# Products of constants in twelve pauses of TensorE, joins moved behind them, and one PSUM bank held aside in block 2

## The reference

```
# block 1: modulation from c, then
h = rms_norm(x) * (1 + sc1) + sh1
proj = h @ w_in                          # attention, GLA and gate parts
att = sliding_window_sink_attention(...) # 8 heads, 2 kv heads, window 128
o = gla_chunked(...)                     # gated linear attention, 4 heads
x = x + gt1 * rms_norm(concat(att, o) @ w_out)
h = rms_norm(x) * (1 + sc2) + sh2
x = x + gt2 * rms_norm(moe_ffn(h))       # 32 experts, top 4
# block 2
z = rmsnorm(x) @ w_in                    # 24 chunks of 128 columns
y_a = rglru_group(...)                   # convolution and linear recurrence
y_b = hgrn2_group(...)                   # gated recurrence, 6 heads of 64, decay per channel
y_c = shortconv_group(...)
x = x + concat(y_a, y_b, y_c) @ w_out
x = x + conv_ffn(rmsnorm(x)); x = x + sigmoid(x @ ple_w_gate) * (p @ ple_w_proj)
x = rmsnorm(x)
# block 3, two layers: swiglu, chunked gMLP or sparse attention (nsa), swiglu, each with a layer norm
```

## Time and profile before

| | |
|---|---|
| median of three runs | 2882.8 us (2879.93 to 2883.49) |
| the profiled execution | 2879.23 us, its span 2877.4 us |
| mean granted clock | 0.963 |
| PE busy | 2691.2 us, 94% of the span |
| DVE busy | 1366.8 us, 48% |
| ACT busy | 941.1 us, 33% |
| DMA | 713.64 MB, mean 248 GB/s |

### The profile page before, as it was taken

How to read it: one execution, slowest core, us unless ns; L and a number is a source line. 1 busy time by engine, 2 the same in 40 slices (tenths; PEclk the granted TensorE clock), 3 DMA queues, 4 the chain that set the end, 5 groups by cost and what they waited for, 6 DMA issues and landing times. The chain is left out here.

```text
span 2877.4 us, 39681 instructions
## 1 busy us (share of the span) xinstructions
PE 2691.2 (94%) x16538; PEld 1868.0 (65%) x16538; DVE 1366.8 (48%) x1958; ACT 941.1 (33%) x1243; POOL 223.4 (8%) x160
## 2 busy tenths in 40 slices
PE   7888999999999999967799989999999999999998
PEld 5654333333233332257699889899889899898897
DVE  3563212222212222267677665566575665664655
ACT  4333111111111111144454443444343444425433
POOL 1200000000000000000000010054020010102200
PEclk9977999999999999988899999999999999989999
DMA  8546999999999999943245556455456466440453
GB/s 289 188 162 254 417 418 416 389 406 416 418 417 382 404 418 416 416 143 112 98 162 191 176 183 200 152 191 176 166 194 200 147 205 199 141 161 31 161 193 115
DMA packets 292703, 713.64 MB, mean 248 GB/s; under 512 B 15587, under 2 KB 189369, under 8 KB 259430
## 3 DMA queue, kind: packets, MB, share of 16 engines
q1 hardware_dynamic: 281168, 690.27, 64.4%
q10 hardware_dynamic: 9734, 17.02, 1.8%
q0 software_dynamic: 1616, 3.74, 0.4%
HBM read 709.93 MB, written 1.05 MB: 247 GB/s over the span
## 5 line engine op out<-in xcount | busy, mean ns | idle before, releaser
L370 DVE TENSOR_TENSOR lo<-ring,hi 128x2048 fp32r<-128x2048 f32 x251 | 597.3, 2384 | 303.7 <-ACT hi L361 303.6
L1818 PE MATMUL bank<-expert,xg 128*64 128x512 f32 x2176 | 510.8, 603 | 23.4 <-DMA expert<-in_w_mlp 22.4
L361 ACT ACTIVATE hi<-ring 128x2048 fp32r<-128x2048 f32 x251 | 475.5, 1897 | 151.1 <-PE bank L639 125.3
L431 PE MATMUL bank<-x_hi,hi 128*128 128x256 f32 x1568 | 382.8, 285 | 0.0
L431 PE MATMUL bank<-x_lo,hi 128*128 128x256 f32 x1568 | 380.2, 281 | 0.0
L1818 PEld LDWEIGHTS bank<-expert,xg 128*64 128x64 f32 x2176 | 142.9, 137 | 315.0 <-issue 269.6
L431 PEld LDWEIGHTS bank<-x_lo,hi 128*128 128x128 f32 x1568 | 295.8, 189 | 2.5 <-issue 1.0
L431 PEld LDWEIGHTS bank<-x_hi,hi 128*128 128x128 f32 x1568 | 294.8, 188 | 3.3 <-issue 1.6
L1915 DVE TENSOR_TENSOR acc<-bank,acc 128x512 f32<-128x512 f32 x136 | 84.4, 682 | 426.6 <-PE bank L1905 426.5
L1888 PE MATMUL bank<-expert,aT 128*64 128x512 f32 x1088 | 244.1, 597 | 3.3 <-DMA expert<-in_w_mlp 3.2
L436 PE MATMUL bank<-x_hi,lo 128*128 128x256 f32 x1568 | 204.0, 282 | 0.0
(11 more groups left out here) (623 smaller groups left out, 3815.7 us busy)
## 6 DMA issues: line engine op xcount, KB each, us to landing
expert<-in_w_mlp SPq DMA_DIRECT2D x384, 1024.0 KB, 16.8
ring<-in_l_ffn_w_in SPq DMA_DIRECT2D x88, 1024.0 KB, 5.1
ring<-in_l_ffn_w_out SPq DMA_DIRECT2D x44, 1024.0 KB, 4.9
ring<-in_w_ada SPq DMA_DIRECT2D x24, 1024.0 KB, 6.5
ring<-in_l_gm_w_in SPq DMA_DIRECT2D x24, 1024.0 KB, 5.1
ring<-in_ffn_w_up SPq DMA_DIRECT2D x22, 1024.0 KB, 5.1
ring<-in_w_in SPq DMA_DIRECT2D x21, 1024.0 KB, 5.4
ring<-in_l_gm_w_out SPq DMA_DIRECT2D x12, 1024.0 KB, 4.9
```

The costliest lines, as they stand in the source:

```text
L361: e.activation(k.half("hi", u), k.slot(j), ACT.Copy).then_inc(*k.up("hi_done"))
L370: e.tensor_tensor(k.half("lo", u), k.slot(k.units[u][0]), k.half("hi", u).bitcast(F32), SUB).then_inc(*k.up("lo_done"))
L431: e.matmul(o, l, r, start=fresh, stop=False, skip_group_check=True)
L1818: i = e.matmul(banks[n][j][h * CAP:(h + 1) * CAP, :], x, W[:, (2 * h + j) * 512:(2 * h + j + 1) * 512], start=c == 0, stop=False, skip_gro ...
```

## The change

`stay_busy_pe` issues n products of the identity with the first 512 (or 448) columns of the constants into a bank that is not in use at that time; they add to no semaphore. They are called fillers below. Their numbers and places:

| place | fillers |
|---|---|
| GLA, level 1, ahead of the wait for the level; ahead of the bank of score (1,1,0) | 2, 7 (of 448 columns, in `mod_bank`) |
| attention, second part of jobs 0 and 1, behind the request of the bank | 6, 4 |
| w_out, ahead of the first unit | 7 |
| norms pre2, mix2, fin2, gm, nsa, behind the request of four banks | 11, 26, 10, 7, 7 |
| HGRN2, behind the wait for "hg in" | 11 |
| HGRN2, level 1, ahead of the wait for the level; ahead of the banks of (1,0,1), (4,0,1), (5,0,1), (6,0,1) | 3, 14, 2, 5, 5 |

The joins post1, post2, fin2, gm and nsa stand behind the fillers now, no longer in front of the requests of banks. In block 2 a bank named `spare` is held from before the first units to the end of the decay scores; one more product closes its use.

```diff
+def stay_busy_pe(k, e, out, n):
+    for _ in range(n):
+        e.matmul(out[:, :], k.cc("ident"), k.t["const"][:, 0:out.shape[1]], start=True, stop=True, skip_group_check=True)
-def turn_rows_pe(k, e, nm, src="unit", done=None):
+def turn_rows_pe(k, e, nm, src="unit", done=None, join=None, busy=0):
     banks = [k.bank(e, nm, "turn", i) for i in range(4)]
+    stay_busy_pe(k, e, banks[0], busy)
+    if join:
+        meet(k, e, PE_, join)
...
             Q, K_ = k.t[f"{nm}qe{li % 2}"], k.t[f"{nm}ke{li % 2}"]
+            stay_busy_pe(k, e, spare, busy.get(li, 0))
             e.wait_ge(*k.dve(nm, "level", li))
         for c in range(n):
             for par in range(2):
                 key = (nm, "score", li, c, par)
+                stay_busy_pe(k, e, spare, busy.get((li, c, par), 0))
                 bank, lo = k.bank(e, *key), par * 64
...
-    decay_pe(k, e, "gla", t["gq"], t["gk"], 2, between)
+    decay_pe(k, e, "gla", t["gq"], t["gk"], 2, between, k.mod_bank[:, 64:512], {1: 2, (1, 1, 0): 7})
...
     bank = k.bank(e, "swa", "pv", job)
+    stay_busy_pe(k, e, bank, (6, 4, 0, 0)[job])
...
+        if i == 0:
+            stay_busy_pe(k, e, acc[0, 0], 7)
         e.wait_ge(*k.dve("mo_parts", "lo", i))
...
-    turn_rows_pe(k, e, "mix2")
+    turn_rows_pe(k, e, "mix2", join="post2", busy=26)
+    k.spare = k.bank(e, "spare", hold=True)
...
     e.wait_ge(*k.dve("hg", "in"))
-    decay_pe(k, e, "hg", t["hq"], t["hk"], 3, between_pe)
+    stay_busy_pe(k, e, k.spare, 11)
+    decay_pe(k, e, "hg", t["hq"], t["hk"], 3, between_pe, k.spare, {1: 3, (1, 0, 1): 14, (4, 0, 1): 2, (5, 0, 1): 5, (6, 0, 1): 5})
+    e.matmul(k.spare[:, :], k.cc("ident"), k.t["const"][:, 0:512]).then_inc(*k.MM("spare"))
+    k.drains[("spare",)] = ("mm_done", k.counts["mm_done"].n)
+    k.release("spare")
...
-    meet(k, e, PE_, "post2")
     block2_pe(k, e)
```

More of the change, by code:

```diff
@@ L814, in decay_act, with decay_pe @@
             between(k, e, li)
-def decay_pe(k, e, nm, q, kk, n, between=None):
+def decay_pe(k, e, nm, q, kk, n, between=None, spare=None, busy={}):
     for li, h in enumerate(LEVELS):
@@ L1456, in mixer_out_pe @@
     acc_free(k, "w_out")
-    meet(k, e, PE_, "post1")
-    turn_rows_pe(k, e, "pre2")
+    turn_rows_pe(k, e, "pre2", join="post1", busy=11)
 def sums_done(k, nm, last=3):
@@ L2532, in conv_ffn_pe @@
     acc_free(k, "ple_gate")
-    meet(k, e, PE_, "fin2")
-    turn_rows_pe(k, e, "fin2")
+    turn_rows_pe(k, e, "fin2", join="fin2", busy=10)
 def conv_ffn_act(k, e):
@@ L2941, in gmlp_pe @@
     acc_free(k, "gm")
-    meet(k, e, PE_, "gm")
-    turn_rows_pe(k, e, "gm")
+    turn_rows_pe(k, e, "gm", join="gm", busy=7)
 def gm_load_act(k, e):
@@ L3490, in nsa_pe @@
     acc_free(k, "nsa")
-    meet(k, e, PE_, "nsa")
-    turn_rows_pe(k, e, "nsa")
+    turn_rows_pe(k, e, "nsa", join="nsa", busy=7)
 def nsa_act(k, e):
```

## The result

The changed kernel takes 2894.12 us (median of seven runs, 2889.86 to 2899.26), the kernel before 2883.35 us (seven, 2879.93 to 2884.79): ratio 1.0047, 95% interval 1.0035 to 1.0059, 10 to 17 us slower. 2892 had been forecast, slower. A second comparison on another chip gave 1.0058 (1.0040 to 1.0076). So the change loses time, although the granted clock rises: the profiled execution took 2894.12 us (span 2892.3) at a mean granted clock of 0.983, against 0.963 before.

What follows compares the result with a forecast made beforehand. PE's pauses leave low-clock stretches, while the PE-busy expert stream shifts whole. Terms -8.8 + 8 + 2 + 9.5 - 0.6 = +10.1 on a median of 2882.8 gave 2892 us; own range 2886 to 2898, overall 2880 to 2904.

Steps and rivals of the forecast that it cites:

- block 1's fillers: GLA level 1, attention, w_out and pre2: a gain of 8.8 us in sum, bounds 5 and 10.9.
- the 26 at mix2: Block 2's norm mix2: fillers start only behind DVE's join and overrun the 11.7 us free; a loss of 8.
- the 11: Block 2, "hg in": they stand behind DVE's wait and fill nothing, later work mostly covers; with level 1's 3, loss of 2.
- the 14: Block 2, level 1, behind the first score's wait: they fill nothing, ACT has 0.9 us slack; a loss of 9.5.
- the 0.50 of the rival: Cheap-filler rival: a filler costs 0.50 us, as L1905's products do, so the change is faster, 2877; chance 0.11.
- I take 4.3: Attention in block 1: the gain from full clock, out of up to 5.1 us, since ACT's copies are also on the path.
- w_out's 1.2: w_out in block 1: fillers end 0.8 us late, products run at full clock; net gain 1.2 us.
- GLA's 1.3: GLA level 1 in block 1: the unit behind the scores runs hot, 6.01 instead of 7.29 us; gain 1.3.
- pre2's 2.0: Norm pre2 in block 1: hot transposes, router and turn save up to 3.3 us, copies leave some 2.0.
- slack hides the decay's fillers: Rival, block 2's decay: ACT's and DVE's slack turns the losses 2 and 9.5 into 0, total 2881; chance 0.17.
- The stream does not keep block 1's gain: Denies the rival that DMA sets MoE's end and keeps block 1's gain, 2902; chance 0.22 together with cold fillers.
- Cold fillers in the decay: Rival, block 2: the decay's fillers run cold, +4.5 us, 2897; chance 0.22 together with the stream keeping the gain.

Runs made afterwards that it cites:

- the fitted run: Changed kernel with 10 fillers at mix2, 8 ahead of the "hg in" wait, level 1, 4 and 6 fillers cut and moved ahead; 0.9971 of the kernel before.
- first pair of traces: First profiled executions of the kernel before (2879.23 us) and of the changed kernel (2894.12 us), read against each other.
- the first four experiments: Against the kernel before: block 1's fillers alone 0.9979; no decay fillers, no held bank 1.0014; held bank alone 1.0004; decay's fillers ahead of waits 1.0034.

## Why the forecast held, step by step

| term | forecast | measured |
|---|---|---|
| block 1's fillers | -8.8 | -6.0 and -5.8 (runs); -5.8 (traces) |
| the 26 at mix2 | +8 | +7.9 (traces); 9 to 12 (runs) |
| the 11 | +2 | +2.1 alone, 0 beside the 14 |
| the 14 | +9.5 | +12.4 to 14.5 (traces); 11 to 14 (runs) |
| held bank, joins | 0 | +1.2 (-2.6 to 4.6) |
| levels 4 to 6, end of decay | 0 | +0.6 (traces) |
| fin2, gm, nsa | -0.6 | +0.3 (traces) |
| whole change | +10.1 | +13.5 and +16.7 |

By the traces the measured terms add up to 17.5 (-5.8, 7.9, 2.1, 12.4, 0.6, 0.3, the bank at 0), a little more than either ratio. The forecast of +10.1 was too low by two terms that err the same way, block 1 by 3 and the 14 by 3 to 5. The forecast median has a slip besides: 2882.8 and 10.1 are 2892.9, not 2892.5.

- **What a filler costs, and where.** Right. The fillers of gm in the changed kernel, with the transposes behind them:

```profile
2103.26 6.17 PE L468 MATMUL bank<-const 128*128 128x512 f32 x14
2109.27 1.27 PE L483 MATMUL bank<-const,unit 128*128 128x128 f32 x8
```

  Seven take 6.01 from start to start, 0.86 each, the value taken from the earlier trace rows; the 0.50 of the rival falls. "In front of the wait or behind it" decided the sign of the block 2 terms.
- **Block 1: sum within its bounds by luck, its parts wrong.** The step that failed is "I take 4.3" for attention: it priced the clock of one execution. Without fillers in it the same part took 27.3 to 34.5 us, with them 29.6 to 34.5: no gain. Two terms of 5.5 us together came to nothing, and one that the prediction does not have made up for some 3 of them. w_out's 1.2 failed too. Its fillers first wait for their bank, as PE's timeline of the changed kernel shows:

```profile
185.55 6.25 PE L468 MATMUL bank<-const 128*128 128x512 f32 x14 [1.12 <-ACT unit L959]
```

  They end 6.8 us behind attention, 1.6 later than the old wait, and spend what the hot clock returns; attention's end to w_out's end is 29.8 to 30.3 us with and without them. GLA's 1.3 held (36.0 instead of 37.2 to 38.1 us from the first scores of level 0 to those of level 4). pre2's 2.0 was a little high for the transposes and the router: from w_out's end to the first expert it is 27.1 to 28.0 us with the fillers and 28.7 to 28.9 without. What it lacked was a term that I hadn't looked for: I had read the expert stream from 288 us on, at clock 1.00, and missed that its first 61 us ran at 0.93. That is worth 2.7 to 4.2 us in eight of the nine traces with block 1's fillers, and nothing in the first trace of the changed kernel, where the clock was at 0.50 from 4.6 us before the expert's start to 5.6 behind it, and again for 3.4 us later.
- **mix2: right** in mechanism and size: the fillers wait for the join, overrun the 11.7 us by 12.8, and hot transposes and units return some 5. That the two waits of the norm's chain take back what a fitted number would give was shown only by the fitted run.
- **The 14: right in mechanism, the term too small** by 3 to 5. It was reckoned with all 14 at full clock. PE idles before the score (2.66 us), and part of the 14 is at half clock: 13.98 us instead of the 12.0 of the sum. The rest is that they began 1.4 us later than I had put them.
- **Levels 4 to 6.** The first pair of traces said +3, six with such fillers against six without say +0.6 (53.5 and 52.9 us from z9's read to w_out_2, where the six without go from 50.3 to 55.7). The 0 stands; that pair would have taught the wrong thing.
- **Transposes.** By the Trainium skill (TensorE: Matmul & The Clock Gate, Part 4: PE-mode transpose) the full clock would not engage for them. Eight took 1.04 us behind the ten fillers of the fitted run, at granted clock 1.00, and 1.94 in the earlier trace rows at 0.50. The trace disagrees with the rule for transposes that find the clock high. Whether transposes alone would bring it up, no run here shows.
- **The rivals.** That slack hides the decay's fillers is false for the 14 and true for the 11. The stream does not keep block 1's gain: 5.8 us at the join are 6.0 at the end. Cold fillers in the decay are true in part: 2.0 us on the 14, where that rival had 4.5 in all.

**Open:** what makes attention take 27 or 34 us in the same kernel. PE's waits for w_ada's transfers before it differ between the executions as the clock does, and no run here separates the two.

## What to carry to other kernels

Idle products that keep the clock up must stand ahead of the wait that they fill, be hardly longer than it, and have work behind them that PE alone bounds. Here 11 of them in front of the norm pre2 and the experts, 1.1 us longer than the old pause, brought 4.3 us (0.9 to 7.8) of the 6 that all of block 1 brought. Ten that fitted the pause in front of a norm bound by ACT and DVE brought nothing, and 26 or 14 too late cost 8 and 12 or more. Judge such a change by the time and never by the clock or by PE's busy share, both of which rise with useless work. And read a phase from several executions before you price it: here one phase moved by 6 us between two executions of one kernel, as much as the effect that was looked for.

## What the runs showed that I had not expected

- **A kernel's own spread goes with its clock.** In the 30 executions of the kernel before beside the first four experiments, the mean granted clock goes from 0.957 to 0.967 and the time from 2886.12 to 2873.05 us: the six slowest had 0.957 to 0.961, the six fastest 0.964 to 0.967. Which of the two drives the other is not shown. Between kernels the relation can be reversed: 0.983 for the profiled execution of the changed kernel at 2894, 0.971 for that of block 1's fillers alone at 2868.
- **How long the clock stays low decides, not whether it falls.** No filler stands between pre2 and the first expert, and PE has short waits there (0.6 to 1.4 us each) with and without fillers. The clock fell to 0.50 in this part in every trace. In six of the nine with block 1's fillers it was back 2.1 to 2.9 us before the expert started, and the expert ran at 1.00; in the other three it stayed low for 10.2 us, into the expert. In all four without them the expert ran at 0.92 or 0.93. The low stretch in the run of block 1's fillers alone, and in the changed kernel, where the expert starts at 243.47 and at 241.44 (columns of the earlier trace rows):

```profile
237.43:240.84 3.41, 3.22 (x8) 0.85 (x8) 1.46 (x10) 0.00 (x0) 0.00 (x0) 0.50 0.03 10
```

```profile
236.81:247.05 10.24, 8.76 (x28) 2.69 (x26) 1.26 (x8) 1.78 (x3) 0.00 (x0) 0.50 0.38 115
```

  Why it was short in six and long in three is open.
- **Two costs that don't add.** 11 fillers in front and 14 behind cost 2.1 and 14.5 us alone and 14.5 together.
